# Scan steps at a group's first and last chunk, and the turning of the second expert block's rows

## The reference

```python
states = einsum('bclgn,bgrcl,bclgrp->bcgrpn', bc, decay_states, x_dt)      # what a chunk adds to the state
states = concatenate([zeros_like(states[:, :1]), states], axis=1)          # chunk 0 starts from a state of zero
states = einsum('bgrzc,bcgrpn->bzgrpn', decay_chunk, states)[:, :-1]       # the last chunk's own is used by nobody
y_off = einsum('bclgn,bcgrpn,bgrcl->bclgrp', cc, states, exp(a_cum))
y = y_diag + y_off
```

## Time and profile before

| | us |
|---|---|
| median of 3 runs (lowest, highest) | 1673.49 (1671.9, 1680.16) |
| the profiled execution | 1674.41 |
| its span, first to last instruction | 1672.7 |
| PE busy | 1591.2 (95%) |
| DVE busy | 1282.3 (77%) |
| ACT busy | 718.7 (43%) |
| POOL busy | 597.3 (36%) |

### The profile page before, as it was taken

How to read it: one execution, slowest core, us unless ns; L and a number is a source line. 1 busy time by engine, 2 the same in 40 slices (tenths; PEclk the granted TensorE clock), 3 DMA queues, 4 the chain that set the end, 5 groups by cost and what they waited for, 6 DMA issues and landing times. The chain is left out here.

```text
span 1672.7 us, 26337 instructions
## 1 busy us (share of the span) xinstructions
PE 1591.2 (95%) x7546; PEld 1288.9 (77%) x7546; DVE 1282.3 (77%) x2333; ACT 718.7 (43%) x1227; POOL 597.3 (36%) x745
## 2 busy tenths in 40 slices
PE   6899999999999999999999895999999999999996
PEld 5778888878878788888888775777777777777774
DVE  6667868858778768788687675787888788878883
ACT  5333222222332223232322342556666666666662
POOL 2221131121131221211311212355666676656564
PEclk9999999999999999999999995899999999999998
DMA  4122121221121121221211473899999999999992
GB/s 154 38 75 56 45 82 32 58 70 38 46 70 45 58 70 32 64 57 48 79 32 45 163 256 110 321 348 337 371 379 373 366 378 373 371 379 367 378 363 71
DMA packets 143296, 292.70 MB, mean 175 GB/s; under 512 B 21644, under 2 KB 72252, under 8 KB 143200
## 3 DMA queue, kind: packets, MB, share of 16 engines
q1 hardware_dynamic: 128208, 266.29, 45.5%
q0 software_dynamic: 14992, 25.22, 4.2%
HBM read 291.81 MB, written 25.30 MB: 190 GB/s over the span
## 5 line engine op out<-in xcount | busy, mean ns | idle before, releaser
L1973 DVE TENSOR_TENSOR gu_lo<-w_gu,gu_hi 128x1024 fp32r<-128x1024 f32 x256 | 307.3, 1223 | 56.8 <-ACT gu_hi L1823 45.8
L1265 PE MATMUL proj<-uTh,wl 128*128 128x512 f32 x768 | 311.7, 406 | 6.8 <-issue 6.8
L1823 ACT ACTIVATE gu_hi<-w_gu 128x1024 fp32r<-128x1024 f32 x256 | 264.9, 1056 | 95.2 <-PE g_ps L1889 44.2
L1267 PE MATMUL proj<-uTh,wh 128*128 128x512 f32 x768 | 303.6, 395 | 0.0
L1266 PE MATMUL proj<-uTl,wh 128*128 128x512 f32 x768 | 302.8, 394 | 0.0
L531 POOL TENSOR_TENSOR wl<-raw,wh 128x512 fp32r<-128x512 f32 x96 | 128.7, 1358 | 392.1 <-ACT wh L625 392.1
L1265 PEld LDWEIGHTS proj<-uTh,wl 128*128 128x128 f32 x768 | 146.7, 191 | 37.4 <-issue 7.4
L1267 PEld LDWEIGHTS proj<-uTh,wh 128*128 128x128 f32 x768 | 146.3, 191 | 32.4
L1266 PEld LDWEIGHTS proj<-uTl,wh 128*128 128x128 f32 x768 | 146.8, 191 | 29.3
L678 ACT ACTIVATE xbc<-v 128x512 f32<-128x512 f32 x64 | 40.5, 632 | 297.5 <-DVE v L985 297.5
L985 DVE SCALAR_TENSOR_TENSOR v<-xr,cw,v 128x512 f32<-128x512 f32 x192 | 146.1, 761 | 15.7 <-DVE v L985 1.5
(11 more groups left out here) (280 smaller groups left out, 3327.1 us busy)
## 6 DMA issues: line engine op xcount, KB each, us to landing
w_gu<-in_moe_w_gate_dram SPq DMA_DIRECT2D x128, 512.0 KB, 17.7
w_gu<-in_moe_w_up_dram SPq DMA_DIRECT2D x128, 512.0 KB, 17.8
w_d<-in_moe_w_down_dram SPq DMA_DIRECT2D x128, 512.0 KB, 17.6
raw<-in_ssd_w_in_dram SPq DMA_DIRECT2D x96, 256.0 KB, 3.4
E<-acum_dram SPq DMA_DIRECT2D x64, 256.0 KB, 3.5
raw<-in_ssd_w_out_dram SPq DMA_DIRECT2D x32, 256.0 KB, 2.9
hacc<-in_x_dram SPq DMA_DIRECT2D x8, 512.0 KB, 7.7
out_dram<-hacc SPq DMA_DIRECT2D x8, 512.0 KB, 5.7
```

What stands on the lines that cost most here:

```text
L1265: nc.tensor.matmul(out, al, bh, start=start, stop=False)
L1267: return nc.tensor.matmul(out, ah, bh, start=False, stop=stop)
L1823: nc.scalar.activation(wh[:, j % RING, :], weights.gate_up(b, j), ACT.Copy).then_inc(w_hi, 1)
L1973: vec.tensor_tensor(wl[:, j % RING, :], weights.gate_up(b, j), wh[:, j % RING, :].bitcast(F32), ALU.subtract).then_inc(w_lo, 1)
```

## The change

Two edits. **In the scan**, chunk 0 of a group has no product with the state and no scaling: DVE copies `y_ps[:, 1]` and `st_ps[:, 0]` instead. The last chunk of a group makes no `btok`, no `xds`, no product for the state and no memsets. Only the counts that the engines wait for are changed with it (`states`, `sums`, `updates`). **In the experts**, for the first pair's block 0 alone (`opening`), the rows of block 1 are turned in the middle of `gate_up` (on PE after piece 3, on ACT and DVE after piece 5) instead of after it, and ACT and DVE make only two pieces of block 1 ahead of silu and the product with up, and the other two behind them.

```diff
+        def states(n):
+            return n if n < NT else n - 1
+        def sums(n):
+            return max(2 * n - 1, 0) - (n > NT)
+        def updates(n):
+            return max(2 * n - 1, 0) - 2 * (n >= NT) - (n > NT)
...
             def copy_b(G, c):
+                if c == NT - 1:
+                    return
...
             def prep(G, c):
-                wait(dve, btok_done, G, NT, c + 1)
+                if c == NT - 1:
+                    wait(dve, tcb_done, G, NT, c + 1)
+                else:
+                    wait(dve, btok_done, G, NT - 1, states(c) + 1)
...
                 vec.tensor_tensor(cbm[:], tp[:, 3, :], tri[:], ALU.mult).then_inc(cbm_done, 1)
-                wait(dve, xdt_steps, G, 2 * NT, 2 * c + 1)
-                wait(dve, st_mm, G, NT, c - 1)
+                if c == NT - 1:
+                    return
+                wait(dve, xdt_steps, G, 2 * NT - 1, c + 1 + states(c))
+                wait(dve, st_mm, G, NT - 1, states(c - 1))
...
             def y_and_state(G, c):
...
-                vec.tensor_tensor(heads(ysb[:]), heads(y_ps[:, 0, :]), spread(eac, G, c), ALU.mult).then_inc(y_steps, 1)
-                wait(dve, y_steps, G, 2 * NT, 2 * c + 1)
-                vec.tensor_tensor(ysb[:], ysb[:], y_ps[:, 1, :], ALU.add).then_inc(y_steps, 1)
+                if c % NT == 0:
+                    vec.tensor_copy(ysb[:], y_ps[:, 1, :]).then_inc(y_steps, 1)
+                else:
+                    ...
+                if c == NT - 1:
+                    return
                 new = S[:, (c + 1) % 2, :]
-                if is_last(G) and last_chunk:
-                    return
-                wait(dve, st_mm, G, NT, c + 1)
-                if last_chunk:
-                    for j in range(2):
-                        vec.memset(new[:, j * P:(j + 1) * P], 0.0).then_inc(s_steps, 1)
+                wait(dve, st_mm, G, NT - 1, states(c + 1))
+                if c % NT == 0:
+                    vec.tensor_copy(new, st_ps[:, 0, :]).then_inc(s_steps, 1)
                     return
...
             def scan(G, c):
-                wait(pe, s_steps, G, 2 * NT, 2 * c)
-                wait(pe, y_steps, G, 2 * NT, 2 * c)
-                nc.tensor.matmul(y_ps[:, 0, :], xbc[...], S[:, c % 2, :], start=True, stop=True)
+                wait(pe, y_steps, G, 2 * NT - 1, sums(c))
+                if cc:
+                    wait(pe, s_steps, G, 2 * NT - 3, updates(c))
+                    nc.tensor.matmul(y_ps[:, 0, :], xbc[...], S[:, c % 2, :], start=True, stop=True)
...
-                if is_last(G) and c == NT - 1:
+                if c == NT - 1:
                     return
...
+        def opening(p, b):
+            return is_pair(p, 0) and b == 0
...
# ACT
+                    early = RING // 2 if opening(p, b) else RING
                     for j in range(RING, 8):
                         split(p, b, j)
+                        if opening(p, b) and j == 5:
+                            turn_x(p, b, 1)
...
-                        for j in range(RING):
+                        for j in range(early):
                             split(*((p, 1) if b == 0 else (shifted(p, 1), 0)), j)
...
                     nc.scalar.activation(hid[:], g_ps[:], ACT.Silu).then_inc(silu_done, 1)
-                    if b == 0 or not last:
+                    for j in range(early, RING):
+                        split(p, 1, j)
+                    if (b == 0 or not last) and not opening(p, b):
                         turn_x(p, b, 1)
...
# PE, in gate_up and in its body
                     mm.then_inc(w_used, 1)
+                    if opening(p, b) and j == 3:
+                        turn_x(p, b, 1)
...
-                    if b == 0 or not last:
+                    if (b == 0 or not last) and not opening(p, b):
                         turn_x(p, b, 1)
...
# DVE
+                    early = RING // 2 if opening(p, b) else RING - 1
                     for j in range(RING, 8):
                         split(p, b, j)
+                        if opening(p, b) and j == 5:
+                            turn_x(p, b, 1)
...
-                        for j in range(RING - 1):
+                        for j in range(early):
...
                     vec.tensor_tensor(hid[:], hid[:], u_ps[:], ALU.mult).then_inc(hid_done, 1)
                     if b == 0 or not last:
-                        split(*((p, 1) if b == 0 else (shifted(p, 1), 0)), RING - 1)
-                        turn_x(p, b, 1)
+                        for j in range(early, RING):
+                            split(*((p, 1) if b == 0 else (shifted(p, 1), 0)), j)
+                        if not opening(p, b):
+                            turn_x(p, b, 1)
```

More of the change, by code:

```diff
@@ L691, in copy_b @@
             def copy_b(G, c):
+                if c == NT - 1:
+                    return
                 wait(act, tcb_done, G, NT, c + 1)
-                wait(act, st_mm, G, NT, c - 1)
+                wait(act, st_mm, G, NT - 1, states(c - 1))
                 nc.scalar.activation(btok[:, c % 2, :], tcb_ps[c % 2][:, 2, :], ACT.Copy).then_inc(btok_done, 1)
@@ L1033, in make_m, with y_and_state @@
                 vec.tensor_tensor(E[:, c % 2], E[:, c % 2], cb, ALU.mult).then_inc(m_done, 1)
-            def y_and_state(G, c, last_chunk):
+            def y_and_state(G, c):
                 wait(dve, y_mm, G, NT, c + 1)
                 wait(dve, yT_done, G, NT, c)
-                vec.tensor_tensor(heads(ysb[:]), heads(y_ps[:, 0, :]), spread(eac, G, c), ALU.mult).then_inc(y_steps, 1)
-                wait(dve, y_steps, G, 2 * NT, 2 * c + 1)
-                vec.tensor_tensor(ysb[:], ysb[:], y_ps[:, 1, :], ALU.add).then_inc(y_steps, 1)
+                if c % NT == 0:
+                    vec.tensor_copy(ysb[:], y_ps[:, 1, :]).then_inc(y_steps, 1)
+                else:
+                    vec.tensor_tensor(heads(ysb[:]), heads(y_ps[:, 0, :]), spread(eac, G, c), ALU.mult).then_inc(y_steps, 1)
+                    wait(dve, y_steps, G, 2 * NT - 1, sums(c) + 1)
+                    vec.tensor_tensor(ysb[:], ysb[:], y_ps[:, 1, :], ALU.add).then_inc(y_steps, 1)
+                if c == NT - 1:
+                    return
                 new = S[:, (c + 1) % 2, :]
-                if is_last(G) and last_chunk:
+                wait(dve, st_mm, G, NT - 1, states(c + 1))
+                if c % NT == 0:
+                    vec.tensor_copy(new, st_ps[:, 0, :]).then_inc(s_steps, 1)
                     return
-                wait(dve, st_mm, G, NT, c + 1)
-                if last_chunk:
-                    for j in range(2):
-                        vec.memset(new[:, j * P:(j + 1) * P], 0.0).then_inc(s_steps, 1)
-                    return
-                wait(dve, s_steps, G, 2 * NT, 2 * c)
+                wait(dve, s_steps, G, 2 * NT - 3, updates(c))
                 vec.tensor_tensor(heads(new), heads(S[:, c % 2, :]), spread(dch, G, c), ALU.mult).then_inc(s_steps, 1)
-                wait(dve, s_steps, G, 2 * NT, 2 * c + 1)
+                wait(dve, s_steps, G, 2 * NT - 3, updates(c) + 1)
                 vec.tensor_tensor(new, new, st_ps[:, 0, :], ALU.add).then_inc(s_steps, 1)
@@ L1304, in tcb @@
                 wait(pe, unit_final, H, NU, 7 if cc < 4 else 8)
-                wait(pe, xdt_steps, G, 2 * NT, 2 * (c - 1))
-                wait(pe, btok_done, G, NT, c - 1)
+                wait(pe, xdt_steps, G, 2 * NT - 1, 2 * (c - 1))
+                wait(pe, btok_done, G, NT - 1, states(c - 1))
                 out = tcb_ps[c % 2]
@@ L1316, in scan @@
                 H, cc = (G, c) if c < 8 else (nxt(G), c - 8)
-                wait(pe, s_steps, G, 2 * NT, 2 * c)
-                wait(pe, y_steps, G, 2 * NT, 2 * c)
-                nc.tensor.matmul(y_ps[:, 0, :], xbc[:, H[1] % 2, 3, cc * P:cc * P + P], S[:, c % 2, :], start=True, stop=True)
+                wait(pe, y_steps, G, 2 * NT - 1, sums(c))
+                if cc:
+                    wait(pe, s_steps, G, 2 * NT - 3, updates(c))
+                    nc.tensor.matmul(y_ps[:, 0, :], xbc[:, H[1] % 2, 3, cc * P:cc * P + P], S[:, c % 2, :], start=True, stop=True)
                 wait(pe, m_done, G, NT, c + 1)
@@ L1324, in scan @@
                 mm.then_inc(y_mm, 1)
-                if is_last(G) and c == NT - 1:
+                if c == NT - 1:
                     return
-                wait(pe, xdt_steps, G, 2 * NT, 2 * c + 2)
-                wait(pe, btok_done, G, NT, c + 1)
+                wait(pe, xdt_steps, G, 2 * NT - 1, c + 2 + states(c))
+                wait(pe, btok_done, G, NT - 1, states(c) + 1)
                 wait(pe, gate_steps, G, 24, 3 * c)
@@ L1332, in turn_y @@
             def turn_y(G, c):
-                wait(pe, y_steps, G, 2 * NT, 2 * c + 2)
-                if not (is_last(G) and c == NT - 1):
-                    wait(pe, s_steps, G, 2 * NT, 2 * c + 2)
+                wait(pe, y_steps, G, 2 * NT - 1, sums(c + 1))
+                wait(pe, s_steps, G, 2 * NT - 3, updates(c + 1))
```

8 lines of the change are left out of this document (4 added, 4 removed).

## The result

The changed kernel took 1655.83 us (median of 4 executions, 1650.94 to 1659.37), the kernel before 1674.53 beside it: ratio 0.9895, 95% interval 0.9870 to 0.9921. The second set of executions (experiment e3) gave 1657.21, ratio 0.9911 (0.9889 to 0.9932): some 16 to 19 us less. The profiled execution took 1650.94, with a span of 1649.2.

A forecast was written before the change was run, and what follows sets the result against it. PE's own list was taken to set the pace, with DVE ahead of the loop; -6.3 - 1.4 - 1.6 + 0.4 = -8.9 us took the profiled 1674.41 to 1665.5, at the median 1664.6 us, range 1661.5 to 1669.5.

The forecast's parts named there:

- The products, -6.3: Scan's groups: PE drops seven products at 0.52 us and seven at 0.40, taken as 6.3 us less.
- rival B: Scan: removed products free less than their distance of starts, as neighbouring loads fill it; 4.2 instead of 6.3, 1666.7 us; chance 0.10.
- The prologue and its clock, -1.4 and -1.6: Ahead of the loop: DVE's two copies start PE's turn 1.4 us earlier; the clock then holds, 1.6 us less.
- I cost this at nothing within the groups: Scan's groups: DVE's and ACT's lighter work at chunk 0 and the last chunk saves nothing, covered by PE's list.
- The experts, +0.4: First expert block: turning rows earlier moves PE's wait to piece 4 of block 1; 0.4 us lost, bounds -0.9 and +2.0.
- A: Clock falls ahead of the loop anyway, or behind PE's wait at piece 4: adds 1.6, giving 1666.2 us; chance 0.24.
- C: Groups: freed time is waited back for ACT's squares, so the 6.3 us fall away, giving 1670.9 us; chance 0.08.
- D: Experts: transfers become the bound, all later blocks at 18.95 us instead of 18.46, giving 1677.8 us; chance 0.04.

The follow-up runs named there:

- e3: The changed kernel run again, unchanged, for a second profile: 1657.21 us, ratio 0.9911 to the kernel before.
- e5: Kernel before with PE's half of the scan's edits alone (products left out, DVE's and ACT's work kept): 1662.58 us, ratio 0.9946.
- e11: Kernel before with DVE's and ACT's edits at chunk 7 alone, memsets kept, PE issuing an unused product: 1671.55 us, ratio 1.0002.
- e6: Kernel before with DVE's and ACT's half of the scan's edits alone, PE still issuing unused products: 1659.52 us, ratio 0.9924.
- e2: Kernel before with the edits of the first expert block alone, none of the scan's: 1672.70 us, ratio 0.9999.
- e8: Changed kernel with DVE's table of extra blocks cut in three, placed around the first and ahead of the second block's hTl: 1650.70 us, ratio 0.9885.
- e12: Kernel before with the loop over pairs of groups written out: 1653.38 us, ratio 0.9896.
- e9: Changed kernel with DVE's table of extra blocks cut in three and the loop over pairs of groups written out: 1644.13 us, ratio 0.9843.

## Why the prediction was wrong

**The products, -6.3: the size came out by luck.** At the ends of seven groups 6 us went. By the starts I priced two products at 0.92 us; e5 shows 0.63 in the first, third and fifth group and 0.47 in the others from chunk 7 to 0, with 0.10 lost behind chunk 0, so some 3.2 us in seven groups, less even than rival B's 4.2. This is rival B's mechanism, though not its reason: the freed time runs into a wait for DVE's mean square. Of the rest, 2.5 us are 0.35 per group from chunk 6 to 7, from DVE's lighter chunk 7 (e11), which the forecast had priced at nothing.

**The prologue and its clock, -1.4 and -1.6: right, the second in part by luck.** The turn came at 110.69 with a wait of 0.78 us for S, forecast 111.3 and 0.9, and 0.6 of the difference was there before the change acts. A copy takes 0.42 us. Behind it:

```profile
111.19:115.19 4.00, 4.00 (x18) 3.29 (x18) 3.47 (x11) 1.70 (x5) 1.75 (x2) 1.00 0.54 167
```

The clock's part is worth 1.6 us only where the clock had fallen behind the wait of 1.78 us, which it did in three profiles of five.

**The step that failed: "I cost this at nothing within the groups: PE's list covers it (788 of 805 us), and DVE has 177 us of slack there."** It priced DVE's and ACT's part of the scan at 0; e6, which has that part alone, took 12.1 us off the groups, of which 2.7 are the prologue's, and so 9.4 us came where nothing was forecast. The slack of 177 us is a sum over the stretch and says nothing of one place. At chunk 0, 1.35 us of DVE's work stood on two paths that the busy shares hide. One goes through PE's sequencer at the loop's turns: 7 us with the clock behind them. One goes through ACT's raisings and the transfers to chunk 3 of the odd groups: 3 us. The row for the first was in the waits of PE, two times 3.4 us for "issue", and I did not price it; for the second the text even named chunk 3 of every odd group as the place of the longer waits, and took it as far from the change.

**The experts, +0.4: too small to be read.** In the changed kernel piece 4 of block 1 began 27.52 us behind the first product (26.9 forecast), and PE waited 1.28 us for DVE's low half there, 0.69 in e3, 2.19 in e2. The three profiles with the edit alone have 27.4 to 27.5 us; the nine without it have 26.8, the first one, to 28.0. So the edit moved PE's wait from the start of the block to piece 4, as forecast, and neither gain nor loss shows. The earlier turn of the rows brings nothing while DVE's table stands there; e8 moves the table and gets 2.3 us of it.

**Rivals.** A's fall at the turn of chunk 0 did not come, nor its fall behind piece 4 in the changed kernel, though e2 has that one. C did not come, and D did not: the later blocks stand 18.46 us apart in both kernels. The forecast lacked a rival in which the change shortens something it does not touch. That its sum of 8.9 us is near what the two kernels differ by once the loop is gone (9.3 from e12 to e9) is partly chance, as e8's edit has a share in the 9.3 and the products gave only half of their term.

## What to carry to other kernels

Another engine's work is covered by the bottleneck engine's queue only as long as the sequencer of that engine does not have to wait for it. At a loop's turn the last wait of the body sets when the sequencer can branch, so price every "issue" row of the bottleneck engine, and ask what it waited for last ahead of it. Write out a loop of few turns where the program can be longer: it was worth as much here as the whole change. Read a relieved engine's path through the chunks behind it (who gets its input sooner, which buffer is freed sooner, which transfer starts sooner) before calling the relief free of effect.

## What the runs showed that I had not expected

Against a step of 11.26 or 11.35 us without it, a turn of the loop costs PE 2.0 to 2.7 us at a clock that holds, 4.1 to 4.7 where the clock falls behind it (e5, e6), and 5.0 to 6.9 where the last wait comes late too. PE's branch at the turn took 3.5 to 4.9 us. A packet of the program's instructions was there at every turn, 2.6 to 3.3 us ahead of the first product of the next body. The granted clock fell behind a stall of 2.30 us and held behind one of 2.49, fell behind a wait of 1.34 and held behind one of 1.37, and did both behind the same 1.78.
